# Second half's first mixer: selections made earlier, sparse queries projected last, sparse attention computed with queries on partitions

## The chip, the cores and the metric
The kernel runs on one core of a Trainium2 chip. The metric is the time of one execution on the device in microseconds (us): three runs of the kernel before took 3576.25 us in the median (3576.12 to 3578.21). The engines are TensorE (PE in the profile, with PEld for its weight loads), VectorE (DVE), ScalarE (ACT), GpSimd (POOL) and SyncE (SP), which issues most DMAs. Each works through its own list in order and waits on semaphores.

## The reference, cut to what matters
A first block of two layers (feed-forward, token mixer, feed-forward) is followed by a second block of two layers (mixer, cross attention, MLP). The change touches only the mixer of the second block's first layer, for 512 tokens and width 1024:

```
qa, ka, va, qb, ckv, qi, ki, wi = split(h @ w_in)
qa, ka = rope(rmsnorm(.)) per head (64 wide);  ki = rope(rmsnorm(ki));  qi = rope(qi)
kb, vb = split(rmsnorm(ckv) @ w_kv_up);  qb, kb = rope(rmsnorm(.)) per head
# dense part: 4 heads, each with two score maps, causal
attn  = softmax(qa0 ka0 / 8) - lam * softmax(qa1 ka1 / 8)
out_a = rmsnorm(attn @ va) * (1 - lam_init)
# sparse part: 8 heads; each query sees the 128 keys with the best index score
# (the loop of 16 rounds of 8 below), among those that are causal
isc   = sum_h relu(qi_h ki) * wi_h ;  idx = top_k(isc)
out_b = softmax(qb kb[idx] / 8) @ vb[idx]
y = concat(out_a, out_b) @ w_out
```

`rmsnorm` divides by the root of the mean square plus 1e-6 and multiplies by a gain per feature.

## The kernel before
Activations lie with features on partitions and the 512 tokens along the free dimension, in eight tiles of 128 features. A projection is computed from weights and activations that are each split in a high and a low part (`s_wh`, `s_wl`, `s_hh`, `s_hl`), with three matmuls for each product. The split of the weights costs ACT a copy (L1912) and DVE a subtraction (L2248) of 128x2048 for each chunk.

A planner (class `Plan`) writes one list of steps; every engine then executes its part of each step in this order. A projection calls `tick()` after each half of an output tile (12 matmuls of 512 columns). A tick advances each unit of background work in `active` by one stage and starts new ones from the queue `bg`, at most `burst` (1, in the sparse part 2), while fewer than `depth` are active and at least `reserve` scratch tiles are spare. `until` and `pipeline` tick with no projection beside. In this mixer `depth` is 7 (10 at the end) and `reserve` 3.

The order in `even_mixer` (L982): the projections of `qi`, `ki` and `wi`; then `qa`, `ka` (eight tiles), `va` with tokens on partitions, the compressed `ckv`, `qb` (four tiles), and the product of the normed `ckv` with `w_kv_up`, which gives `kb` and `vb`. The normed `ckv` is written into the tiles of `h` itself (`ck_part`), so it waits until the projection of `qb`, the last reader of `h`, has ended. The background queue holds in this order:
- `index` (L2660 to L2676): for the query blocks i = 1, 2, 3 the index scores of (i+1)*128 keys; 16 rounds of MAX8 (`ix_top`, L2669) and MATCH_REPLACE8 (L2671), which take out the eight best keys of each query at a time; and a mask `bm`. Block 1 does two rounds a tick, blocks 2 and 3 one round.
- `group(1)`, for `qa` and `ka`: `g_rs` computes the roots of eight heads' mean squares for each of `qa` and `ka` by Newton steps on DVE (L2224 to L2236). `g_turn` transposes them (L1804). For each of the eight tiles `g_scale` spreads the roots over the features with one PE matmul (`s_rt`) and multiplies them in on DVE (L2640); `e_rope` then turns the tile (PE, POOL L2898, DVE L2645 and L2647). `group(2)` does the same for `qb` and `kb`, once both are projected.
- 16 dense units (`a_unit`), 4 heads by 4 query blocks: two score matmuls (`s_ka`, `s_qa`), DVE adds the causal mask and takes the maximum (L2688), ACT computes exp and the sum (L2126). `ea_mix` takes two reciprocals, scales one map by its reciprocal (L2699) and adds the other (L2703). Then come transposes on PE (L1574), a copy on ACT and the product with `va`.
- `a_norm`: the mean squares of the dense output, roots, and their application (L2724).
- 32 sparse units (`attend`), in the order of head pair, query block, head: one score matmul of 64 rows (`s_kb`, `s_qb`); DVE adds the mask and takes the maximum (L2522); ACT computes exp and the sum (L2076); DVE takes the reciprocal (L2528) and scales the map (`at_norm`, L2530); PE transposes (L1574), ACT copies (L1912). In `at_av` PE multiplies by `vb`: the 64 features of a head are the stationary operand, 128 queries stream, and two heads of a pair write the lower and the upper 64 partitions of one bank. When a pair's four blocks are done the bank is split into the tiles 4 to 7 of `h` (ACT L1912, DVE L2241). The projection by `w_out_e` reads the tiles of `h` in the order 0 to 7.

Of the kernel before, what the change touches and what calls it, by code (L numbers as in the profile page):

```python
# [18 lines left out]
F32 = mybir.dt.float32  # L19
# [86 lines left out]
class Plan:  # L106
# [825 lines left out]
    def attend(self, kind, l, h, i, n, cell, last, free=None, sr=None):  # L932

        u = (kind, l, h, i)
        b, q, sm = self.banks.take(), self.tmp.take(), self.small.take()
# [3 lines left out]
        self.add("at_norm", u, n, q, sm)  # L939
        self.small.free(sm, ("at.n", u))  # L940
        yield
# [10 lines left out]
        if last:  # L952
            o = cell[0]
            if kind == "x":
                self.held.free(o, ("o.lo", l, h), ("o.hi", l, h))
            else:
                self.held.free(o, ("h.lo", self.hv, 4 + h // 2), ("h.hi", self.hv, 4 + h // 2))
# [24 lines left out]
    def even_mixer(self, norm):  # L982
        extra = [("xe", 0)]
        pend = []
# [21 lines left out]
        def proj(idx, key, t0, col, stat=True, eager=False):  # L1006
            ch = self.take("w_in_e", idx)
            for t, (b, pid) in enumerate(self.feat2(ch, 8, "h", hv, eager)):
                if t == 0:
                    flush()  # L1010
                self.add("e_copy", key, t0 + t, pid, b)
                if stat:
# [20 lines left out]
        def group(gid, n, tiles, turns=None):  # L1033
            y = self.yr.take()
# [7 lines left out]
            self.yr.free(y, ("g.t", gid))  # L1042
# [3 lines left out]
            for tile in turns or tiles:  # L1046
# [8 lines left out]
            yield  # L1055

# [11 lines left out]
        for i in extra:  # L1068
            self.tmp.after[i] = [free]
        self.tmp.ids += extra  # L1070
        self.reserve, self.depth = 3, 7
        self.add("e_begin")
        parts = []
# [31 lines left out]
        def index():  # L1105
            for i in (1, 2, 3):
# [22 lines left out]
        small = self.small.take()  # L1129
        self.add("e_gains", small)  # L1130
        for i, key in enumerate(("qa", "ka")):
            for c in range(2):
                proj(2 * i + c, key, 2 * c, 8 * i + 4 * c)
        for c in range(2):
            ch = self.take("w_in_e", 8 + c)
            for i in (0, 2):
# [3 lines left out]
                if i + c:  # L1140
                    continue
                flush()
                self.bg.append(group(1, 16, [(key, n) for key in ("qa", "ka") for n in range(4)],
                                     [(key, n) for n in range(4) for key in ("qa", "ka")]))
# [4 lines left out]
        def a_unit(h, i, cell):  # L1149
# [6 lines left out]
            self.add("ea_score", h, i, b, q, s)  # L1156
            yield
            self.add("ea_mix", h, i, q, s)
# [27 lines left out]
        proj(6, "ckv", 0, 0)  # L1186
        sq, pend[:] = list(pend), []
        held = []

        def compressed():  # L1190
            b = self.banks.take()
            self.add("ck_stat", [q for q, *_ in sq], b)
            for q, *_ in sq:
                self.tmp.free(q, ("ck.st",))
            yield
            y = self.yr.take()
            self.add("ck_rs", b, y, ew)
            self.banks.free(b, ("rs.v", "ck"))
            yield
            b, qs = self.banks.take(), [self.tmp.take(), self.tmp.take()]  # L1200
            self.add("ck_scale", y, b, qs)
            self.yr.free(y, ("ck.sp",))
            self.banks.free(b, ("ck.q", 1))
            yield
            held.extend(qs)

        self.active.append(compressed())
        for c in range(2):
            self.hfree = proj(4 + c, "qb", 2 * c, 4 * c)
        self.until(lambda: held)  # L1210
        self.hv += 1
        for k, q in enumerate(held):
            self.add("ck_part", k, q, self.hv, self.hfree)
            self.tmp.free(q, ("h.lo", self.hv, k), ("h.hi", self.hv, k))
        ch = self.take("w_kv_up", 0)
        cv = self.hv

        def vup(i):
            b, pid = self.toks(ch, 2, 1024, [i], "h", cv, 512, 512)
            self.add("e_vb", i, pid, b)  # L1220
# [4 lines left out]
        for n in range(4):  # L1225
            b, pid = self.feat(ch, 2, 1024, n, "h", cv)
# [4 lines left out]
            self.tick()  # L1231
        vup(0)
# [2171 lines left out]
```

## Time and profile before

| | |
|---|---|
| median of 3 runs | 3576.25 us (3576.12 to 3578.21) |
| profiled execution | 3573.11 us, span 3571.8 us |
| mean granted clock of TensorE | 0.983 |
| PE busy | 3463.5 us (97%) |
| DVE busy | 1880.2 us (53%) |
| ACT busy | 1189.9 us (33%) |
| POOL busy | 505.4 us (14%) |

The span runs from the first to the last instruction. The busy time of PE is modelled; the granted clock says in tenths or as a share of 1 which part of the full TensorE clock the chip granted. The mixer in question lies at about 2140 to 2470 us of the span.

### The profile page before, as it was taken

The page shows a single profiled execution, that of the slowest core. Times are in us where ns is not written, and L with a number is a line of the kernel's source. Part 1 is how long each engine was busy: PE and PEld are TensorE (multiplying, and loading weights), DVE is VectorE, ACT ScalarE, POOL GpSimd, SP SyncE. Part 2 cuts the span into 40 slices and gives each one's busy share as a digit, 9 for nine tenths or more (in the row PEclk, how much of TensorE's full clock was granted, in tenths as well). Part 3 has the DMA queues.
Part 4 walks back from the last instruction along what each step waited for, and adds up shares of the span by engine and source line. Part 5 has one row for each costly group of instructions (what it writes and reads, how often), then busy time and mean ns, then how long its engine had stood idle before and what let it go on. Part 6 is the DMA issues. An engine that isn't in the chain of part 4 may idle for free. (4 is left out here: it accounts for less than half of the span.)

```text
span 3571.8 us, 40973 instructions
## 1 busy us (share of the span) xinstructions
PE 3463.5 (97%) x16684; PEld 2814.3 (79%) x16684; DVE 1880.2 (53%) x3253; ACT 1189.9 (33%) x1611; POOL 505.4 (14%) x436
## 2 busy tenths in 40 slices
PE   8999989999999999999999999989999999999999
PEld 5888876788888888866788887656888888878887
DVE  5545745464556545745652345786554444564333
ACT  3222444342225222444342234235432222352221
POOL 1010212110012010211210021111111110211111
PEclk9999999999999999999999999989999999999999
DMA  6444221134442444321132212101222222322221
GB/s 263 176 173 177 101 77 60 59 118 153 158 149 106 153 153 159 105 73 54 69 134 99 97 66 83 56 16 48 83 83 95 95 95 96 111 75 90 102 94 71
DMA packets 56111, 377.56 MB, mean 106 GB/s; under 512 B 6897, under 2 KB 7025, under 8 KB 13170
## 3 DMA queue, kind: packets, MB, share of 16 engines
q1 hardware_dynamic: 55922, 374.93, 29.3%
q8 instruction: 132, 2.16, 0.2%
q14 instruction: 57, 0.47, 0.0%
HBM read 368.61 MB, written 2.10 MB: 104 GB/s over the span
## 5 line engine op out<-in xcount | busy, mean ns | idle before, releaser
L1554 PE MATMUL ps<-s_hh,s_wh 128*128 128x512 f32 x2488 | 992.6, 399 | 27.2 <-DVE s_xr L2303 10.5
L1554 PE MATMUL ps<-s_hh,s_wl 128*128 128x512 f32 x2488 | 977.1, 393 | 0.0
L1554 PE MATMUL ps<-s_hl,s_wh 128*128 128x512 f32 x2488 | 976.5, 392 | 0.0
L2248 DVE TENSOR_TENSOR s_wl<-s_stage,s_wh 128x2048 fp32r<-128x2048 f32 (+1 forms) x276 | 623.6, 2259 | 665.9 <-ACT s_wh L1912 665.8
L1912 ACT ACTIVATE s_wh<-s_stage 128x2048 fp32r<-128x2048 f32 (+1 forms) x276 | 519.1, 1881 | 600.2 <-PE ps L1554 456.5
L1554 PEld LDWEIGHTS ps<-s_hh,s_wh 128*128 128x128 f32 x2488 | 472.3, 190 | 146.8 <-issue 28.2
L1554 PE MATMUL ps<-s_ah,s_wh 128*128 128x512 f32 x1408 | 561.0, 398 | 0.3 <-POOL s_al L2864 0.3
L1554 PEld LDWEIGHTS ps<-s_hh,s_wl 128*128 128x128 f32 x2488 | 471.7, 190 | 101.1
L1554 PE MATMUL ps<-s_ah,s_wl 128*128 128x512 f32 x1408 | 549.1, 390 | 0.0
L1554 PEld LDWEIGHTS ps<-s_hl,s_wh 128*128 128x128 f32 x2488 | 472.7, 190 | 96.8 <-issue 1.2
L1554 PE MATMUL ps<-s_al,s_wh 128*128 128x512 f32 x1408 | 548.6, 390 | 0.0
L2864 POOL TENSOR_TENSOR s_al<-s_tmp,s_ah 128x512 fp32r<-128x512 f32 x152 | 197.4, 1301 | 1679.5 <-ACT s_ah L1912 1679.4
L1554 PEld LDWEIGHTS ps<-s_ah,s_wl 128*128 128x128 f32 x1408 | 263.7, 187 | 57.4
L1554 PEld LDWEIGHTS ps<-s_ah,s_wh 128*128 128x128 f32 x1408 | 264.1, 188 | 53.9 <-issue 1.4
L1554 PEld LDWEIGHTS ps<-s_al,s_wh 128*128 128x128 f32 x1408 | 264.2, 188 | 53.7 <-issue 1.9
L1912 ACT ACTIVATE s_ah<-s_tmp 128x512 fp32r<-128x512 f32 x152 | 95.9, 632 | 569.6 <-DVE s_tmp L2428 307.4
L2305 DVE TENSOR_TENSOR s_xr<-ps,s_xr 128x512 f32<-128x512 f32 x96 | 66.2, 689 | 197.1 <-PE ps L1554 197.0
L2264 DVE SCALAR_TENSOR_TENSOR s_tmp<-s_stage,s_cond,s_tmp 128x256 f32<-128x256 f32 x381 | 156.3, 478 | 0.0
L2303 DVE SCALAR_TENSOR_TENSOR s_xr<-ps,s_sm,s_xr 128x512 f32<-128x512 f32 x112 | 83.2, 748 | 115.7 <-PE ps L1554 115.1
L1940 ACT ACTIVATE s_tmp<-ps 128x512 f32<-128x512 f32 x82 | 48.9, 596 | 260.5 <-PE ps L1554 260.5
L2428 DVE TENSOR_TENSOR s_tmp<-s_tmp,ps 128x512 f32<-128x512 f32 x82 | 55.6, 685 | 117.5 <-PE ps L1554 116.3
L2412 DVE TENSOR_TENSOR s_tmp<-ps,s_c 128x512 f32<-128x512 f32 x64 | 44.1, 688 | 119.3 <-PE ps L1554 105.4
(489 smaller groups left out, 3720.6 us busy)
## 6 DMA issues: line engine op xcount, KB each, us to landing
s_stage<-in_w_ada SPq DMA_DIRECT2D x64, 1024.0 KB, 4.8
s_stage<-in_ffn_w_gate SPq DMA_DIRECT2D x44, 1024.0 KB, 4.8
s_stage<-in_ffn_w_up SPq DMA_DIRECT2D x44, 1024.0 KB, 4.8
s_stage<-in_ffn_down SPq DMA_DIRECT2D x32, 1024.0 KB, 4.8
s_stage<-in_w_up SPq DMA_DIRECT2D x32, 1024.0 KB, 4.8
s_stage<-in_down_m SPq DMA_DIRECT2D x32, 1024.0 KB, 4.7
s_stage<-in_w_in SPq DMA_DIRECT2D x24, 1024.0 KB, 4.8
s_stage<-in_ffn_down SPq DMA_DIRECT2D x16, 768.0 KB, 4.3
```

The lines of the kernel that those rows point to most:

```text
L1554: return pe.matmul(out, lhs, rhs, start=start, stop=stop, skip_group_check=True)
L1912: return act.activation(out, src, ACT.Copy)
L1940: act.activation(m.tmp(q), m.bank(b), ACT.Silu).then_inc(*e.up("act_ffn", "act", pid))
L2248: ins = dve.tensor_tensor(m.wl(ws)[:, a:z], m.STAGE[:, j % NS, a:z], m.wh(ws)[:, a:z].bitcast(F32), ALU.subtract)
L2264: ins = dve.scalar_tensor_tensor(dst, w[:, k, :], cond, dst, ALU.mult, ALU.add)
L2303: ins = dve.scalar_tensor_tensor(x, m.bank(b), m.small(gate[0])[:, n:n + 1], x, ALU.mult, ALU.add)
L2305: ins = dve.tensor_tensor(x, m.bank(b), x, ALU.add)
L2412: dve.tensor_tensor(x, m.bank(b), m.RB, ALU.mult).then_inc(*e.up("dve_act", "act", pid))
L2428: dve.tensor_tensor(m.tmp(q), m.tmp(q), m.bank(b), ALU.mult).then_inc(*e.up("dve_ffn", "glu", pid))
L2864: pool.tensor_tensor(m.AL[a][:, k, :], m.tmp(q), m.AH[a][:, k, :].bitcast(F32), ALU.subtract).then_inc(*e.up("pool_a", "a.lo", av, k))
```

## The change
The units' stages change, and the order of the projections. The rest of the kernel is the same.

```diff
 even_mixer (planner)
+        early = [("xv", k) for k in range(4)]        # the four tiles of vb as scratch, until vup
-        self.reserve, self.depth = 3, 7
+        self.reserve, self.depth = 4, 12             # and no self.depth = 10 later
         index:
                     self.add("ix_top", i, r, s)
-                    if i > 1 or r % 2:
+                    if r % 2:
                         yield
         order of projections
-        qa, ka, va (group 1 queued after its first half), ckv, qb, [ck_part], kb, vb, group(2: qb+kb)
+        qa, ka, ckv, [group 1 queued], va, [ck_part], kb, vb, group(2: kb), qb, queries()
         def queries():
+            self.add("g_rs", 3, 8, None, list(st["ev"]), ew)
+            done["minus"] = True
         def turned(tile):                            # for qa and qb, right after the copy
+            yield
+            rope(tile, ("e.p", *tile))
         b_units
-            for pr in range(4):
-                for i in range(4):
-                    for c in range(2):
-                        yield self.attend("b", 0, 2 * pr + c, i, (i + 1) * P, cell, ...)
+            for i in range(4):
+                for h in range(8):
+                    yield self.attend("b", 0, h, i, (i + 1) * P, cell, h == 7, sr=bs)
         attend
-        self.add("at_norm", u, n, q, sm)             # and its stage, for "b" only
+            elif kind == "b":                        # after the eighth head of a block
+                yield
+                self.add("b_norm", i, o, sr, q)
+                yield
+                self.add("b_turn", i, q, b)
+                self.add("b_out", i, b, self.hv, free or self.hfree)
 PE
+        if u[0] == "b":   # at_av: the transposed map is stationary, vb streams
+                ins = mul(m.bank(o)[:, 64 * u[2]:64 * u[2] + 64], m.tmp(p)[:, j * P:(j + 1) * P], m.v_of(u, j), ...)
+    def b_turn(i, q, b):
+        turn(m.bank(b), m.tmp(q), S).then_inc(*e.up("pe_turn", "b.t", i))
 ACT
+        if key in ("qa", "qb"):                      # e_copy
+            ins = act.activation(m.tile(key, t), m.bank(b), ACT.Identity, scale=m.small(gains[0])[:, at:at + 1])
+    def b_out: copy(m.HH[:, 4:8, i * P:(i + 1) * P], m.bank(b)...)
 DVE
     g_rs: groups 1 and 3 also write minus = -roots of the queries
     at_score, ea_score: tensor_tensor_reduce(..., ALU.add, ALU.min)
-      scale -1.0
+      scale m.minus(...)                             # minus the query's root, one number per partition
     ea_mix
-        dve.reciprocal(s0[:, 3:4], s0[:, 2:3])
-        dve.tensor_scalar(a0, a0, s0[:, 3:4], None, ALU.mult)
-        dve.tensor_tensor(s1[:, 4:5], s1[:, 3:4], m.LAM[:, 0:1], ALU.mult)
+        dve.tensor_scalar(s1[:, 4:5], s1[:, 3:4], m.LAM[:, 0:1], total, ALU.mult, ALU.mult)
     an_rs: eps becomes 1e-6 times the square of the sum (one instruction more)
+    def b_norm(i, o, sm, q):
+        dve.reciprocal(rc, rc)                       # 8 sums
+        dve.tensor_tensor(q, bank(o), rc broadcast over 64 columns, ALU.mult)
+    def b_out: dve.tensor_tensor(m.HL[:, 4:8, i * P:(i + 1) * P], m.bank(b), m.HH[...], ALU.subtract)
 memory
     the normed ckv goes to the place of qb (QBR) instead of the tiles of h
```

So `qa` and `qb` are no longer multiplied by their roots: the gain is applied in ACT's copy, the tile is turned at once, and the root comes in at the scores. The maps aren't normalized; a block's output of eight heads is multiplied by the reciprocal sums once, then transposed (four transposes) into the tiles 4 to 7 of `h`. Sparse units wait for `kb`, for `minus` and for the mask of block 1, and from block 2 on for their own mask; before they waited for the mask of block 2, and the first of block 3 for that of block 3.

## Rows read from the trace of the kernel before

**Rows 1.** Page, part 1: busy time, share of the span, instructions of each engine.
```profile
PE 3463.5 (97%) x16684; PEld 2814.3 (79%) x16684; DVE 1880.2 (53%) x3253; ACT 1189.9 (33%) x1611; POOL 505.4 (14%) x436
```
**Rows 2.** Stages: window, length, busy PE, PEld, DVE, ACT, POOL; clock, DMA share, GB/s.
```profile
2177.00:2214.00 37.00, 37.00 (x175) 29.22 (x173) 15.37 (x39) 18.16 (x26) 10.95 (x8) 0.91 0.16 57
2214.00:2297.00 83.00, 81.28 (x440) 59.98 (x440) 63.16 (x154) 26.22 (x47) 11.98 (x8) 1.00 0.18 63
2297.00:2357.00 60.00, 52.59 (x257) 39.69 (x253) 35.39 (x105) 26.03 (x56) 0.00 (x0) 0.89 0.11 37
2357.00:2430.00 73.00, 58.99 (x228) 34.28 (x228) 64.63 (x191) 22.72 (x65) 11.91 (x10) 0.77 0.00 1
2430.00:2469.00 39.00, 35.51 (x282) 23.56 (x280) 28.01 (x109) 27.22 (x83) 3.91 (x3) 1.00 0.00 1
2177.00:2469.00 292.00, 265.37 (x1375) 186.73 (x1373) 206.55 (x596) 120.35 (x277) 38.75 (x28) 0.91 0.10 33
```
**Rows 3.** Timeline 2293 to 2333: start, us, engine, line, instruction, idle before and releaser.
```profile
2299.55 0.72 ACT L2126 ACTIVATE s_tmp<-s_tmp,s_sm 128x512 f32<-128x512 f32 x1 [7.38 <-DVE s_sm L2688]
2302.09 0.50 PE L1554 MATMUL ps<-s_hh,s_wh 128*128 128x512 f32 x1 [4.39 <-ACT s_tmp L2107]
2329.45 0.48 PE L1554 MATMUL ps<-s_hh,s_wh 128*128 128x512 f32 x1 [2.51 <-DVE s_hl L2241]
```
**Rows 4.** Busy time in stretches of 2.5 us, columns as in rows 2.
```profile
2330.00:2332.50 2.50, 2.50 (x9) 2.04 (x8) 1.56 (x1) 1.30 (x2) 0.00 (x0) 0.50 0.00 0
2475.00:2477.50 2.50, 2.50 (x13) 2.07 (x12) 0.00 (x0) 1.99 (x7) 1.04 (x2) 1.00 0.97 338
```
**Rows 5.** PE timeline: start, us, instruction; each with the one that follows.
```profile
2384.54 1.12 PE L1554 MATMUL ps<-s_rt,s_c 16*128 16x512 f32 x2
2385.59 1.12 PE L1554 MATMUL ps<-s_qb,s_cc 128*128 128x512 f32 x2
2386.55 1.05 PE L1554 MATMUL ps<-s_tmp,s_va 128*128 128x128 f32 x8
2387.44 0.38 PE L1574 MATMUL ps<-s_cc,s_xe 128*128 128x128 f32 x2
2408.15 1.05 PE L1554 MATMUL ps<-s_cc,s_xe 128*128 128x1 f32 x8 [1.20 <-ACT s_xe L2148]
2409.13 0.49 PE L1554 MATMUL ps<-s_kb,s_qb 64*128 64x128 f32 x4
2454.91 1.36 PE L1574 MATMUL ps<-s_cc,s_ka 128*128 128x128 f32 x8 [0.61 <-DVE s_ka L2530]
```
**Rows 6.** Instructions on `vb` alone, 2177 to 2469: PE, PEld, ACT, clock.
```profile
2177.00:2469.00 292.00, 15.12 (x160) 11.49 (x160) 2.34 (x4) 0.91 0.10 33
```
**Rows 7.** DVE line 2530 alone, 2177 to 2469.
```profile
2177.00:2469.00 292.00, 12.38 (x32) 0.91 0.10 33
```
**Rows 8.** DVE line 2699 alone, 2177 to 2469.
```profile
2177.00:2469.00 292.00, 7.14 (x16) 0.91 0.10 33
```
**Rows 9.** DVE by line and form, 2177 to 2469: busy, mean ns, idle before.
```profile
L2669 DVE MAX8 s_sm<-s_bm 128x8 f32<-128x512 f32 x16 | 11.0, 690 | 0.1
L2671 DVE MATCH_REPLACE8 s_bm<-s_sm,s_bm 128x512 f32<-128x512 f32 x16 | 10.8, 676 | 0.0
L2528 DVE RECIPROCAL s_sm<-s_sm 128x1 f32<-128x1 f32 x32 | 5.1, 159 | 2.8 <-ACT s_tmp L2076 1.6 <-ACT s_ka L2076 0.9 <-ACT s_qi L2076 0.3
L2640 DVE SCALAR_TENSOR_TENSOR s_qb<-s_qb,s_sm,ps 128x512 f32<-128x512 f32 x4 | 3.0, 738 | 0.0
L2241 DVE TENSOR_TENSOR s_hl<-ps,s_hh 128x512 fp32r<-128x512 f32 x3 | 2.1, 692 | 4.1 <-ACT s_hh L1912 4.1
```
**Rows 10.** Timeline: the last of the 12 DVE instructions of a chain of roots.
```profile
2422.29 0.17 DVE L2236 SCALAR_TENSOR_TENSOR s_ny<-s_nu,s_ny 128x16 f32<-128x16 f32 x1
```
**Rows 11.** ACT by line and form, 2409 to 2469.
```profile
L2076 ACT ACTIVATE s_ka<-s_ka,s_sm 128x128 f32<-128x128 f32 x4 | 1.6, 394 | 0.8 <-DVE s_sm L2522 0.8
L1912 ACT ACTIVATE s_tmp<-ps 128x128 f32<-128x128 f32 x6 | 1.3, 262 | 0.0
```

More of the change, by code:

```diff
@@ L934, in attend @@
         u = (kind, l, h, i)
-        b, q, sm = self.banks.take(), self.tmp.take(), self.small.take()
+        b, q, sm = self.banks.take(), self.tmp.take(), sr if kind == "b" else self.small.take()
         self.add("at_score", u, n, b, q, sm, sr)
@@ L1031, in root, with group @@
             done["ew"] = True
-        def group(gid, n, tiles, turns=None):
-            y = self.yr.take()
+        def group(gid, n, tiles):
+            y = self.yr.take() if gid == 0 else None
             self.add("g_rs", gid, n, y, list(st["ev"]) if gid else [("e.stt", 0)], ew)
@@ L1045, in group @@
             prev = None
-            for tile in turns or tiles:
+            for tile in tiles[4:] if gid == 1 else tiles:
                 b = self.banks.take()
@@ L1055, in group, with turned @@
             yield
+        def turned(tile):
+            yield
+            rope(tile, ("e.p", *tile))
         def rope(tile, before):
@@ L1133, in even_mixer, with compressed @@
                 proj(2 * i + c, key, 2 * c, 8 * i + 4 * c)
+        proj(6, "ckv", 0, 0)
+        sq, pend[:] = list(pend), []
+        held = []
+        self.bg.append(group(1, 16, [(key, n) for key in ("qa", "ka") for n in range(4)]))
+        def compressed():
+            b = self.banks.take()
+            self.add("ck_stat", [q for q, *_ in sq], b)
+            for q, *_ in sq:
+                self.tmp.free(q, ("ck.st",))
+            yield
+            y = self.yr.take()
+            self.add("ck_rs", b, y, ew)
+            self.banks.free(b, ("rs.v", "ck"))
+            yield
+            b, qs = self.banks.take(), [self.tmp.take(), self.tmp.take()]
+            self.add("ck_scale", y, b, qs)
+            self.yr.free(y, ("ck.sp",))
+            self.banks.free(b, ("ck.q", 1))
+            yield
+            for k, q in enumerate(qs):
+                self.add("ck_part", k, q)
+                self.tmp.free(q, ("c.lo", 0, k), ("c.hi", 0, k))
+            held.extend(qs)
+        self.active.append(compressed())
         for c in range(2):
@@ L1184, in even_mixer @@
         self.bg.extend(a_units())
[L1186 to L1207, printed above, removed]
-        for c in range(2):
-            self.hfree = proj(4 + c, "qb", 2 * c, 4 * c)
         self.until(lambda: held)
[L1211 to L1214, printed above, removed]
         ch = self.take("w_kv_up", 0)
-        cv = self.hv
+        self.tmp.ids = [i for i in self.tmp.ids if i not in early]
         def vup(i):
-            b, pid = self.toks(ch, 2, 1024, [i], "h", cv, 512, 512)
-            self.add("e_vb", i, pid, b)
+            b, pid = self.toks(ch, 2, 1024, [i], "c", 0, 512, 512)
+            self.add("e_vb", i, pid, b, self.tmp.after["xv", i])
             self.banks.free(b, ("vb", i))
@@ L1231, in even_mixer, with queries @@
             self.tick()
+        self.until(lambda: not self.tmp.busy.intersection(early))
         vup(0)
         flush()
-        self.active.append(group(2, 16, [(key, n) for key in ("qb", "kb") for n in range(4)]))
+        self.active.append(group(2, 8, [("kb", n) for n in range(4)]))
         for i in (1, 2, 3):
-            self.hfree = vup(i)
-        self.release(ch, self.hfree)
+            last = vup(i)
+        self.release(ch, last)
+        for c in range(2):
+            self.hfree = proj(4 + c, "qb", 2 * c, 4 * c)
+        flush()
+        def queries():
+            yield
+            self.add("g_rs", 3, 8, None, list(st["ev"]), ew)
+            st["ev"].clear()
+            done["minus"] = True
+        self.active.append(queries())
         self.hv += 1
@@ L1536, in up, with same @@
         return (self.book.sems[sem], by) if self.live else (None, by)
+    def same(self, event, *others):
+        for other in others:
+            self.book.at[other] = self.book.at[event]
 def xe(n, v):
@@ L2504, in at_score @@
     def at_score(u, n, b, q, sm, sr):
-        mx, nm = m.small(sm)[:, 0:1], m.small(sm)[:, 1:2]
-        e.wait_ge(("at.s", u), sm.after)
+        mx, nm = m.small(sm)[:, 0:1], m.max_sum(u, sm)[0]
+        e.wait_ge(("at.s", u), [("b.n", u[3] - 2)] if u[0] == "b" and u[3] > 1 else sm.after)
         if u[0] == "x":
```

213 lines of the change are left out of this document (136 added, 77 removed).

## The prediction, made before the change was run
> **What bounds the kernel now.** I read the page's busy times first: PE is busy for 97% of the span, DVE for 53%, ACT for 33% [rows 1]. So only PE's work, its pauses and its clock count. The table by stage [rows 2] says where the mixer differs: of the 292 us from 2177 to 2469 PE is busy for 265.4, so 26.6 are pauses, and the clock is below 1 in three of five stages. Busy time times the missing share of the clock is lost as well. By stage, pauses plus clock: 0 + 3.3 us, 1.7 + 0, 7.4 + 5.8, 14.0 + 13.6, 3.5 + 0. That is 49.3 us; the work itself, at the full clock, is 242.7 us. The reader is to see how the stages differ: from 2214 to 2297 DVE works for 76% of the time and PE loses 2%; from 2357 to 2430, with no projection left, DVE works for 89% and PE loses 27.6 of 73 us.
>
> The timeline [rows 3] shows how a busy DVE reaches PE: at 2299.55 ACT had waited 7.38 us for a maximum of DVE (behind a weight split, selections and a root chain), and PE, whose banks ACT empties, stood for 4.39 us. The second pause of this kind, 2.51 us before 2329.45, is the wait for the parts of `ckv`, which may overwrite `h` only after the last `qb` matmul. Right behind it the clock is at 0.50, the lower of its two levels, 1.2 GHz [rows 4].
>
> **PE's work.** (1) The spreading matmuls of `qa` and `qb` go: eight, each 1.05 us from its start to the next (2384.54 to 2385.59) [rows 5]: -8.4 us. (2) The 80 products with `vb` (160 records) keep their number; they took 15.1 us [rows 6], 0.094 us a record, because two heads share the array in halves of its columns. After, 128 columns are stationary, 64 stream, and nothing runs beside it. The trace has no such form. Its neighbours with 128 stationary columns take 0.11 us a record with 128 streaming (0.89 us for eight) and 0.12 with one (0.98 for eight) [rows 5]: 17.8 to 19.6 us. If only the stream counted, half of 0.11 would give 8.9 us. The two neighbours agree although their streams differ by 128 times, so the load decides; I take 18.6: +3.5 us (-6.2 to +4.5). (3) New are 16 transposes, 0.15 us each (eight in 1.36 with their drain) [rows 5]: +2.4 us. Work after: 242.7 - 8.4 + 3.5 + 2.4 = 240.2 us.
>
> On (2) the Trainium skill, TensorEngine Tiling (Array Packing), section "Performance Considerations", speaks against the change: with a streaming side of at most 64 one should swap the operands and tile the columns twice, which is what the kernel before does. Its factor of two would make 30.2 us of the 15.1; it is the last rival below.
>
> **DVE's work.** Removed: the 32 scalings of sparse maps, 12.4 us [rows 7], their 32 reciprocals, 5.1 [rows 9]; the 16 dense scalings, 7.1 [rows 8], with 16 reciprocals of 0.16, 2.5; eight applications of roots at 0.738, 5.9 [rows 9]. Together 33.0. Added: four output norms (0.69 for 128x512, by the split's row, and 0.16), 3.4 us; a third chain of roots, twelve instructions of 0.17 to 0.21, 2.4 [rows 10]; three small ones, 0.6. The four splits of the output replace four of the same size. The multiply by `minus` replaces an immediate in the same instruction: taken as 0; at most one small instruction of 0.16 for each of 64, 10 us of DVE. Net -26.6: 206.6 becomes 180 us, against 240 of PE.
>
> ACT gets a gain in a copy that it makes anyway, at nothing: it is busy for 120 of 292 us [rows 2], and even 0.1 us for each of eight is hidden behind the tile's own matmuls. POOL's part of the turning is unchanged and only comes earlier. SP issues nothing more; weight chunks are read in another order.
>
> **The order, up to the sparse part.** Without the sparse part (80 transposes 12.5, products 18.6, the new turns 2.4, scores some 12: pairs of 128 columns take 0.41 to 0.45, those of 512 about 1; together 45 us) PE has 195 us. DVE has 160 (180 less some 14 for maxima, estimated from the scalings' 12.4 at the same widths, and 6 for norms and splits): 82%, between the two stages above, which lost 2% and 38%. What changes the mix: two rounds of selection a tick instead of one, so `index` takes 30 ticks instead of 46 and ends before `qb` is projected, whose four tiles load PE but hardly DVE; the queries are turned without waiting for roots; `ckv` no longer waits for `qb`, so the pause of 2.51 us and most of the 5.8 us of clock behind it go. Against it: the two rounds of block 3 take 2 x (0.690 + 0.676 + the 0.09 load) = 2.9 us of DVE a tick [rows 9], while a half tile takes PE 12 x 0.227 = 2.7 (2.5 us hold 11 new matmuls and two that reach in) [rows 4]; and the ticks beside `kb` and `vb` are shorter than that. Over some 180 us I take a loss of 9%, 16 us, where it was 42.5; the bounds are 2% and what it was, 3.6 to 42.5. The 3.3 us before 2214 stay.
>
> **The sparse part.** It starts when `qb`'s last tile is copied, squared (0.6 us each), summed, rooted (2.4) and negated; the first units then need DVE and ACT once. Some 7 us, of which turning the last tile and late dense units cover 2: 5 us of pause that was not there (0 to 10). What is queued behind it is everything on PE, and `w_out_e` waits for that. Blocks 0 and 1 come as eight small units each. For block 0 ACT needs 0.394 for exp, 0.1 for the sum that is not overlapped and 0.262 for the copy, 0.76 a unit [rows 11], PE 0.6 (score 0.22, transpose 0.15, product 0.23): 1.3 us over eight; for block 1, with PE at 1.08 (0.32, 0.30, 0.46), they are equal. I take 3 us for both. In the large blocks PE waited for the scaling (0.61 at 2454.91 [rows 5]), which goes: 2.5 us of pauses instead of 3.5. The last `b_turn` waits for `b_norm` with nothing between: 0.69 and two signals, 1.2 us; earlier ones have the next block's units. The copy and subtraction behind the last turn, 0.6 and 0.69 us, lie beside the matmuls on tiles 0 to 3 of `h`, 24 x 0.227 = 5.4 us; if `a_norm` were late, they would cost 1.5 us.
>
> **Sum.** 240.2 + 3.3 + 16 + 5 + 3 + 2.5 + 1.2 = 271.2 us for 292: -20.8. The profiled execution took 3573.11 us, its span 3571.8, the median is 3576.25; taken from the median, this is 3555.5: I predict 3556 us.
>
> **Rivals.** (A) *DVE no longer holds PE at all.* For it: 76% of DVE cost PE only 2% [rows 2]. Against it: DVE's work is still bunched where index, dense units and `kb` meet. The loss is 5 us, the pause 2: 257.2 us, -35: 3541.
> (B) *The bunching moves and stays.* The selections, twice as dense, meet the weight splits, the turning and the dense units, and ACT waits for maxima as at 2299.55 [rows 3]. For it: 2.9 against 2.7 us a tick. Against it: DVE has 26.6 us less. The loss is 33 us instead of 16, all else as in the sum: 288, -4: 3572.
> (C) *Slower: PE runs dry at the start of the sparse part and stays at the low clock.* The selections being done early, nothing is left to fill the root chain; PE stands for 10 us, and the small units of blocks 0 and 1, PE work of 13.4 us in bursts, run at 1.2 GHz and take as much again. For it: the clock was 0.50 behind the pause at 2329 [rows 4] and 0.77 over the stage of short bursts [rows 2]. Against it: the dense units, five ticks long, reach into the `qb` projection. With 25 us lost earlier: 240.2 + 3.3 + 25 + 10 + 16.4 + 3.7 = 298.6, +6.6: 3583. It decides from 18 us of earlier loss on.
> (D) *The products with `vb` cost twice.* 30.2 us instead of 18.6, all else as in the sum: -9: 3567. Against it: eight records with 128 stationary columns took 0.89 us.
>
> **How the numbers follow.** Forecast 0.42, A 0.20, B 0.18, C 0.12, D 0.08. What this kernel's measurement can tell from no change is 0.2%, 7 us. Forecast and A are faster, as are 0.05 of B and half of D: 0.71. The rest of B and D is the same: 0.17. C is slower: 0.12. The range runs from A, 3541, to just past B, 3575, and leaves out C and the lower edge of A. The forecast's own range, with half of each unknown, is 3547 to 3565.
>
> **What would show it.** Right: `s_rt` spreads nine tiles instead of seventeen; records on `vb` stay 160 at 0.11 us and start one after the other; DVE falls by about 27 us; the last MAX8 lies more than 30 us before the first sparse score; no pause before the `kb` matmuls, and one of about 5 us behind the last `qb` matmul. Wrong: pauses plus lost clock between 2214 and the sparse part above 25 us, a low clock in blocks 0 and 1, or records on `vb` above 0.15 us.

## The result, and the profile after

The changed kernel takes 3592.4 us in the median of five runs (3591.5 to 3593.6), the kernel before 3577.1 beside it: a ratio of 1.0043, interval 1.0033 to 1.0054. It is slower by 15.3 us; the prediction was 3556 and faster. The profiled execution of the kernel before (3573.11 us) was quicker than its median by 4 us, so the two profiles lie 18.6 us apart, 3 more than the medians.

The page of the changed kernel, part 1, answers to [rows 1]:

```profile
PE 3464.7 (96%) x16684; PEld 2826.3 (79%) x16684; DVE 1865.4 (52%) x3171; ACT 1193.2 (33%) x1611; POOL 504.8 (14%) x436
```
The span is 3590.4 us, 18.6 longer, and PE is busy for 1.2 us more: the time went into pauses. The stages of the changed kernel, columns as in [rows 2]; the sparse part starts at 2422, the first projection matmul behind it at 2484.6 (2409 and 2469.1 before):

```profile
2178.00:2214.00 36.00, 34.17 (x166) 26.10 (x165) 19.09 (x44) 18.54 (x26) 15.70 (x11) 0.97 0.17 59
2214.00:2287.00 73.00, 71.30 (x412) 57.27 (x411) 55.61 (x136) 20.46 (x33) 6.91 (x5) 1.00 0.16 59
2287.00:2345.00 58.00, 42.48 (x172) 26.13 (x171) 49.31 (x129) 21.33 (x48) 2.53 (x2) 0.85 0.10 37
2345.00:2422.00 77.00, 56.20 (x258) 40.20 (x258) 42.23 (x116) 26.63 (x66) 7.60 (x6) 0.83 0.04 14
2422.00:2484.60 62.60, 59.62 (x380) 45.94 (x379) 26.91 (x92) 36.54 (x105) 5.08 (x4) 0.86 0.00 1
2177.00:2484.60 307.60, 264.77 (x1385) 196.45 (x1385) 193.45 (x516) 124.49 (x279) 37.81 (x28) 0.89 0.09 31
```
From 2287 to 2422, dense units beside the last projections, PE stands for 36 of 135 us. The longest pauses of PE there, from its timeline (columns as in [rows 3]), and one of ACT:

```profile
2295.72 1.87 PE L1585 MATMUL ps<-s_cc,s_tmp 128*128 128x2 f32 x8 [4.36 <-ACT s_tmp L2163]
2335.78 2.07 PE L1585 MATMUL ps<-s_rt,s_c 8*128 8x512 f32 x2 [4.41 <-DVE s_kb L2719]
2338.26 0.51 ACT L2183 ACTIVATE s_ki<-s_ki,s_sm 128x256 f32<-128x256 f32 x1 [7.95 <-DVE s_sm L2767]
2347.42 0.80 PE L1585 MATMUL ps<-s_hh,s_wh 128*128 128x512 f32 x1 [5.47 <-ACT s_tmp L2163]
2368.39 0.77 PE L1585 MATMUL ps<-s_hh,s_wh 128*128 128x512 f32 x1 [6.42 <-ACT s_xe L2163]
2396.04 1.86 PE L1585 MATMUL ps<-s_cc,s_ki 128*128 128x2 f32 x8 [4.54 <-ACT s_ki L2163]
2408.92 0.47 PE L1605 MATMUL ps<-s_cc,s_tmp 128*128 128x128 f32 x1 [5.14 <-DVE s_tmp L2778]
2421.24 1.05 PE L1585 MATMUL ps<-s_cc,s_tmp 128*128 128x1 f32 x8 [1.20 <-ACT s_tmp L2205]
```
Four of them end with ACT's square of a projected tile (L2163, `e_sq`): the first among the `kb` matmuls, two directly ahead of query matmuls (`s_hh`, `s_wh`), whose bank ACT had not emptied, and the one at 2396.04 behind the last query matmul, for the sums of the last query tile. The timeline of all engines ahead of 2368.39, in order:

```profile
2358.68 0.69 DVE L2748 MAX8 s_sm<-s_bm 128x8 f32<-128x512 f32 x1
2361.00 0.68 DVE L2750 MATCH_REPLACE8 s_bm<-s_sm,s_bm 128x512 f32<-128x512 f32 x1
2361.70 1.26 POOL L2979 TENSOR_TENSOR s_qb<-s_qb,s_c 128x512 f32<-128x512 f32 x1
2362.31 1.20 DVE L2726 TENSOR_TENSOR s_kb<-s_kb,s_tmp 128x512 f32<-128x512 f32 x1
2364.14 0.69 DVE L2726 TENSOR_TENSOR s_qb<-s_qb,s_tmp 128x512 f32<-128x512 f32 x1
2365.25 0.75 DVE L2778 SCALAR_TENSOR_TENSOR s_qi<-s_ki,s_sm,s_qi 128x512 f32<-128x512 f32 x1
2365.92 0.34 DVE L2767 CUSTOM_DVE_ANT_0 s_tmp<-ps,s_cc,s_minus 128x128 f32<-128x128 f32 x1
2366.31 0.40 ACT L2183 ACTIVATE s_tmp<-s_tmp,s_sm 128x128 f32<-128x128 f32 x1 [5.09 <-DVE s_sm L2767]
2367.10 0.67 ACT L2156 ACTIVATE s_qb<-ps,s_sm 128x512 f32<-128x512 f32 x1
2367.67 0.58 ACT L2163 ACTIVATE s_xe<-ps 128x512 f32<-128x512 f32 x1
```
This is one step of the plan. DVE does two rounds of block 3 (2358.7 to 2361.6), the turning of a key and of a query tile (behind POOL), a mix, and then the dense maxima, 7.2 us after the step began. ACT waits 5.09 us for them, does the exponentials, and only then the copy and square of the query tile; PE had gone idle at 2361.97.

The pause of 5.14 us before 2408.92 has another length of list ahead of it. The selections have long ended (last MAX8 at 2373.8). PE waits for the mix of a dense unit, and that stands on DVE behind the root chain of the queries, 2.9 us from its first instruction to the end of `minus`:

```profile
2405.23 0.18 DVE L2695 TENSOR_TENSOR s_nv<-s_st,s_sm 128x32 f32<-128x32 f32 x1
2407.92 0.18 DVE L2707 TENSOR_SCALAR s_minus<-s_roots 128x32 f32<-128x32 f32 x1
2408.51 0.35 DVE L2778 SCALAR_TENSOR_TENSOR s_tmp<-s_tmp,s_sm 128x128 f32<-128x128 f32 x1
```

For each kernel I added up windows of 1 us, from 2177 to the first matmul of `w_out_e`: idle is length less busy, lost clock is busy time by the missing share of the clock, work is the rest.

| mixer | idle | lost clock | work of PE | DVE busy | rest of the kernel, lost clock |
|---|---|---|---|---|---|
| before (292.1 us) | 26.6 | 24.6 | 240.9 | 206.5 | 5.1 |
| changed (307.6 us) | 42.8 | 25.9 | 238.9 | 193.5 | 8.3 |

The pauses (+16.2) are the result. PE's work fell by 2.0, 1.3 more of clock were lost in the mixer, and 3.2 more behind it.

### The profile page after: what moved, and what is told of

Its sections match the earlier page's. It is cut to its first block, busy times and chain, and to the rows that moved or that the text cites. A ratio compares the mean times of both kernels' runs of the same rounds, so it can differ in the third digit from the quotient of the medians.

```text
span 3590.4 us, 40926 instructions
## 1 busy us (share of the span) xinstructions
PE 3464.7 (96%) x16684; PEld 2826.3 (79%) x16684; DVE 1865.4 (52%) x3171; ACT 1193.2 (33%) x1611; POOL 504.8 (14%) x436
## 4 chain that ended last, share of the span: by engine, by line
PE 44%; DVE 4%; ACT 1%; issue 1%; POOL 0%; DVEq 0%; ACTq 0%; POOLq 0%
PE ps L1585 43%; PE ps L1605 1%; DVE s_bm L2750 0%; DVE s_sm L2748 0%; DVE s_wl L2305 0%; ACT s_wh L1954 0%; ACT s_tmp L2118 0%; DVE s_xr L2434 0%; DVE s_tmp L2767 0%; DVE s_sm L2565 0%; DVE s_hl L2298 0%; ACT s_xx L2118 0%; DVE s_na L2287 0%; DVE s_nu L2289 0%; DVE s_tmp L2424 0%
## 5 line engine op out<-in xcount | busy, mean ns | idle before, releaser
L1585 PEld LDWEIGHTS ps<-s_ah,s_wh 128*128 128x128 f32 x1408 | 264.9, 188 | 53.7 <-issue 1.4
```

The lines of the kernel that those rows point to most:

```text
L1585: return pe.matmul(out, lhs, rhs, start=start, stop=stop, skip_group_check=True)
```

## The experiments

Five runs or more for each, all beside the kernel before (3576.7 to 3577.9 us in the comparisons). "Late" is the change's order (queries last), "early" has the queries ahead of the expansion.

**One selection round a step (late, new form).**
```diff
-                    if r % 2:
+                    if i > 1 or r % 2:
```


> The changed kernel with one round of selections a step of the plan for blocks 2 and 3 (two for block 1), as the kernel before had it. Everything else is the change's: queries last, new order, folded factors, new sparse form. (The row buffer of the sparse maxima and sums lies in a place of its own, as one buffer more is then in use.) Theory D, the dense: the added idle time (42.8 us against 26.6 between 2177 and the last projection) comes from two selection rounds (2.9 us for block 3) standing in VectorE's queue ahead of the dense maxima of the same step, ScalarE waiting for those maxima with the eviction of a query projection behind it, and TensorE behind that. Then this kernel is 8 to 15 us faster than the changed one: 3577 to 3584 us. Theory O, the order of the projections: the pauses come from the late query projections lying beside the dense units, whatever the selections do: 3590 to 3596 us. Theory S, the new sparse form costs it: 3592 us, within 2.


3581.5 us, ratio to before 1.0014 (1.0005 to 1.0023): 11 us less than the changed kernel. Mixer: idle 30.1, clock 26.1. So two rounds do cost, in this order. (The sparse maxima and sums got a row buffer of their own here, as one buffer more is in use at a time.)

**Selections last in a step.**
```diff
-        self.active = [u for u in self.active if next(u, "end") != "end"]
+        order = [u for u in self.active if u is not last] + [u for u in self.active if u is last]
+        self.active = [u for u in order if next(u, "end") != "end"]
```


> The changed kernel with the unit that issues the selections advanced last in each step of the plan, so that VectorE has the dense maxima and mixes of a step ahead of its two selection rounds. Same work, same number of steps. Theory D: most of the 16 us of added idle time goes, 3578 to 3584 us. Theory O: no more than 3 us, 3589 to 3592 us. Theory S: 3592 us. Slower, 3595 us or more, if what ends last after all are the selections of block 3, which then come later.


3587.4 us, 1.0030 (1.0018 to 1.0041): 5 us less than the changed kernel. Idle 36.2. A part, smaller than expected; that the next step's maxima then stand behind them may be why, which no run tells.

**The old sparse form and order (late).** `attend`, `at_norm`, `at_turn`, `at_av` and `b_units` as before, scale `minus` kept.
```diff
-                ins = mul(m.bank(o)[:, 64 * u[2]:...], m.tmp(p)[:, j * P:...], m.v_of(u, j), ...)
+                ins = mul(m.o_of(u, o), m.v_of(u, j), m.tmp(p)[:, j * P:...], ...)
```


> The changed kernel with the sparse units of the kernel before: rows normed one by one (reciprocal and multiply on VectorE), value products with features on partitions, four pairs of heads one after another, no turn of the outputs. The queries' scale stays with the maximum. Theory S, the new form of the products (21.2 us of TensorE against 15.1, 16 turns more, low clock in the sparse part 8.5 us against 6.5) costs what was lost: 3577 to 3582 us. Theories D and O: the loss was before the sparse part, so that this one is as slow as the changed kernel or slower by the 13 us of VectorE's work that comes back where VectorE bounds: 3590 to 3604 us.


3585.1 us, 1.0022 (1.0013 to 1.0031): 7.3 us less than the changed kernel. PE's work in the mixer is 233.2 instead of 238.9, idle unchanged (43.6), although DVE has 13.5 us more. So the new form costs its work on PE, and what it spares DVE is worth nothing. The edit undoes the swap, the 16 turns and the order by blocks together; no run parts them. The products' weight loads and matmuls, first of the changed kernel, then of this one (duration in ns: least, median, most):

```profile
L1585 PEld LDWEIGHTS ps<-s_vb,s_ka x46: 186/192/333, 2434.9 to 2480.9; 128*128 128x128 f32 x46
L1585 PE MATMUL ps<-s_vb,s_ka x46: 222/275/421, 2435.1 to 2481.0; 128*128 128x64 f32 x46
```
```profile
L1571 PEld LDWEIGHTS ps<-s_ka,s_vb x64: 132/137/231, 2437.3 to 2478.7; 128*64 128x64 f32 x64
L1571 PE MATMUL ps<-s_ka,s_vb x64: 272/273/476, 2437.3 to 2478.8; 128*64 128x128 f32 x64
```
The matmuls last the same with half the stream; the load of 128 columns takes 192 ns instead of 137, and the tile is the whole array. Over a run of each kind, from the timelines of both:

```profile
2460.74 1.45 PE L1585 MATMUL ps<-s_vb,s_tmp 128*128 128x64 f32 x12
```
```profile
2457.14 1.36 PE L1571 MATMUL ps<-s_ka,s_vb 128*64 128x128 f32 x14
```
From the start of each run to the start of what follows it that is 0.108 us a record (2460.74 to 2462.03, twelve) against 0.094 (2457.14 to 2458.65, sixteen in all), both at the full clock.

**Queries early (new form, two rounds).** The projection of `qb` and `queries()` move ahead of `w_kv_up`; the split `ckv` goes to `h` again.
```diff
+        for c in range(2):
+            self.hfree = proj(4 + c, "qb", 2 * c, 4 * c)
+        flush(); self.active.append(queries())
         self.until(lambda: held)
+        self.add("ck_part", k, q, self.hv, self.hfree)     # into h
         kb, vb, group(2: kb)
-        qb, queries()
```


> The changed kernel with the sparse queries projected ahead of the expansion of the compressed part, as in the kernel before, the split compressed part back in the normed input's place. Two selection rounds a step, folding and new sparse form stay. The dense units can then start beside the query projections (16 of 16 scored by the end of the projections' last value tile but 6, against 9). Theory O: 3576 to 3583 us. Theory D: two rounds a step lie ahead of the dense maxima as before, 3588 to 3593 us. Theory S: 3592 us.


3574.3 us, 0.9993 (0.9984 to 1.0002): 18 us less than the changed kernel, though `ckv` waits for the queries again. Idle 29.6, clock 19.5. With two rounds, the order is the largest part.

**Early, with one round; then with the old form; then old form with two rounds.**


> Queries projected ahead of the expansion and one selection round a step for blocks 2 and 3; folding and the new sparse form stay. Queries early alone gave 3574.3 (18 us less than the changed kernel), one round alone 3581.5 (11 less). If the two causes are separate (theory O and D both true), this kernel takes 3564 to 3570 us. If both are one cause, a step overfull beside the late query projections, the second step adds little: 3572 to 3576 us. Slower than 3576 us if the selections of block 3, drawn out again, now end last before the sparse units of that block.

> As the last, and the sparse units in their old form and order: what is left of the change is the folding of the factors into the exponents and maxima, the values' space lent as scratch, and the late maxima waiting for the factors. Old form alone saved 7.3 us on the changed kernel (5.7 us less TensorE work). Theory S as an additional, separate cost: 6 to 8 us less than the last one, 3558 to 3564 us. If VectorE bounds instead (13.5 us of its work come back), no less than the last one: 3566 to 3572 us. The kernel before takes 3576.7.

> As the last but with two selection rounds a step for blocks 2 and 3. It says what the early selections alone do once order and sparse form are the old ones: theory D 4 to 10 us slower than the last one (3564 to 3572), theory of one cause 0 to 2 us slower.


3581.3, 3576.9 and 3563.5 us; to before 1.0010 (1.0002 to 1.0019), 1.0001 (0.9993 to 1.0010), 0.9962 (0.9948 to 0.9975). One round is slower here than two (by 7 us with the new form, by 13 with the old); of what I had written down only the last case of the first expectation allowed for it. The two causes are not separate. Two rounds, early and the old form beat both kernels.

**The kernel before with two rounds.**
```diff
-                    if i > 1 or r % 2:
+                    if r % 2:
```


> The kernel before with one edit: two selection rounds a step for blocks 2 and 3, which brings the last selection from step 57 of the plan to step 42. VectorE's work is the same 206.5 us. Theory D (bunched selections ahead of the dense maxima hold ScalarE and TensorE back): 3580 to 3588 us against 3576.7. Prediction's view (the selections go into time in which TensorE has work of its own, the loss shrinks): 3568 to 3574 us.


3587.3 us, 1.0026 (1.0015 to 1.0037), 10 us slower: with nothing else of the change, early selections lose, as the rival to the prediction's view had it. Its longest pauses:

```profile
2310.26 0.79 PE L1554 MATMUL ps<-s_hh,s_wh 128*128 128x512 f32 x1 [6.86 <-ACT s_tmp L2107]
2348.26 0.77 PE L1554 MATMUL ps<-s_hh,s_wh 128*128 128x512 f32 x1 [8.71 <-DVE s_hl L2241]
```
They are the two of [rows 3], 4.39 and 2.51 us there. These two grew by 8.7 us, but other pauses shrank: over the mixer idle is 28.9 (2.3 more), lost clock 28.5 (3.9 more) and the busy time at full clock 245.0 (4.1 more, with the same matmuls, which nothing here explains). So the pauses alone are not the 10 us.

**The late order with the old form and one round.**


> The changed kernel with the old sparse form and one round a step. It fills the last corner: late or early queries, one or two rounds, with the old form. With the new form late queries cost nothing at one round (3581.5 against 3581.3). Theory V says the same here: 3573 to 3580 us against 3576.9 with early queries. If the equality was chance, late queries cost 5 us or more here too: 3582 us and up.


3574.0 us, 0.9992 (0.9983 to 1.0001). The corners (medians, us):

| | late, two rounds | late, one | early, two | early, one |
|---|---|---|---|---|
| new form | 3592.4 (the change) | 3581.5 | 3574.3 | 3581.3 |
| old form | 3585.1 | 3574.0 | 3563.5 | 3576.9 |

Late costs 18 and 22 us with two rounds, 0 and -3 with one. The new form costs 4 to 11 us in each column.

Where the time is lost, from the same windows of 1 us (pauses + lost clock, us). The cut is at the last projection matmul ahead of the sparse units: of `vb` in the kernel before and in the early ones, of `qb` in the late ones.

| | 2214 to the last projection | from there to the first sparse score | sparse part |
|---|---|---|---|
| before | 10.7 + 6.7 | 7.9 + 7.9, in 45.1 us | 8.0 + 6.5 |
| the change (late, two) | 26.0 + 9.5 | 12.0 + 6.2, in 34.2 us | 3.0 + 8.5 |
| late, one (new form) | 9.1 + 6.0 | 14.7 + 9.9, in 45.1 us | 4.6 + 9.2 |
| early, two (new form) | 20.3 + 9.2 | 3.7 + 0.0, in 22.2 us | 3.0 + 8.5 |
| early, one (new form) | 15.6 + 11.1 | 7.0 + 4.7, in 34.0 us | 5.1 + 8.9 |

Two rounds in the late order lose ahead of the last projection (20.4 us more than one) and give 6.4 back behind it. The late order with two rounds loses 6.0 us ahead of it and 14.5 behind it, where the last query tile's square, the root chain and the dense units' rest stand one behind the other; with one round the late order also costs 12.9 there, but gives 11.6 back ahead of it. Dense units move across this cut from kernel to kernel, so that the table says where the loss lies and not what each unit costs.

**Is it room for dense units to start?** `self.reserve` 2 instead of 4 in the changed kernel; and no lent scratch (`early = []`) in the 3563.5 kernel.


> The changed kernel, queries late, with one number changed: a new unit starts when 2 scratch tiles are free (the change asks for 4). By the last query matmul step 14 dense units have had their scores instead of 11, and the sparse units begin 2 steps earlier. Theory P (pacing: what the early queries bought was room for dense units to start, 18 us): 3574 to 3582 us, near the kernel with early queries. Theory O (the late query projections, whose evictions and squares stand in ScalarE's queue behind dense exponentials, are the pauses themselves): 3588 to 3595 us, the five pauses of 4.4 to 6.4 us stay.

> The fastest so far (early queries, old sparse form, two rounds a step: 3563.5 us) without the four scratch tiles lent from the values' place, so that 9 instead of 13 dense units have their scores by the end of the projections. Theory P: 8 to 15 us slower, 3572 to 3578. Theory O: order alone did it, within 3 us, 3561 to 3567.


3591.5 us, 1.0041 (1.0027 to 1.0055), and 3564.5 us, 0.9965 (0.9953 to 0.9978). Neither made the difference that pacing would. `depth` 12 instead of 7 was not tried alone.

**The keys out of the query steps (late, two rounds).**
```diff
-        self.active.append(group(2, ...kb))        # after vup(0)
+        self.active.append(group(2, ...kb))        # after the projection of qb
```


> The changed kernel, queries late and two rounds, but the roots, scaling and rotation of the sparse keys begin when the query projections have ended instead of beside them. Open: why late queries cost 18 us with two rounds and nothing with one. Theory V (a step's queue on VectorE is too long: beside a query projection it holds two rounds of block 3, 2.9 us, the scaling and rotation of a key tile, the rotation of a query tile, and only then the dense maxima; the pauses of 4.4 to 6.4 us end with the square behind those maxima): without the keys in it the steps are 2 to 3 us shorter, and this kernel takes 3576 to 3584 us. Theory Q (the queries' own evictions and squares behind dense exponentials are enough): 3589 to 3596 us, or more, as the keys now come last.


3589.9 us, 1.0037 (1.0025 to 1.0050): 2.5 us less than the changed kernel. That is far from theory V and within what theory Q said. Its pauses:

```profile
2331.62 0.47 PE L1605 MATMUL ps<-s_cc,s_tmp 128*128 128x128 f32 x1 [4.07 <-DVE s_tmp L2778]
2358.15 0.48 PE L1605 MATMUL ps<-s_cc,s_ki 128*128 128x128 f32 x1 [5.82 <-DVE s_ki L2778]
2383.24 1.86 PE L1585 MATMUL ps<-s_cc,s_tmp 128*128 128x2 f32 x8 [4.53 <-ACT s_tmp L2163]
```
The two pauses ahead of the query matmuls, 11.9 us, are gone, but others came, of transposes that wait for DVE's mixes: idle 36.0 (6.8 less) and clock 28.8 (2.9 more). Without the keys in those steps the two pauses do not occur, but nearly half of their length comes back elsewhere, and behind the last query matmul 11.8 us of pauses and 7.9 of clock are lost (12.0 and 6.2 in the changed kernel).

**Only block 3 with one round (late, new form).** `if i == 3 or r % 2`; the dense and projection steps stay what they are.


> The changed kernel with one round a step for block 3 alone. The other work falls into the same steps of the plan as in the changed kernel, step by step up to the sparse units; only the 32 selections of block 3 (22 us of VectorE) lie over 16 steps instead of 8, and end ahead of the sparse units. It is the cleanest test of the two rounds: if they, queued ahead of the dense maxima beside the query projections, cost the 11 us that one round for both blocks gave back, 3578 to 3584 us, with the two pauses of 5.5 and 6.4 us ahead of the query matmuls under 3 us each. If it was block 2's rounds, or room for other units: 3588 to 3593 us.


3584.6 us, 1.0022 (1.0013 to 1.0031): 7.8 us less than the changed kernel, with nothing moved up to the sparse units but the 16 rounds of block 3 (a row buffer of its own, as in the one-round kernel, beside it). Idle 35.7. The two pauses ahead of the query matmuls are

```profile
2340.30 0.80 PE L1584 MATMUL ps<-s_hh,s_wh 128*128 128x512 f32 x1 [3.41 <-ACT s_tmp L2162]
2360.94 0.76 PE L1584 MATMUL ps<-s_hh,s_wh 128*128 128x512 f32 x1 [5.86 <-ACT s_xe L2162]
```
3.41 (5.47) and 5.86 (6.42) us: the first lost some of its length, the second hardly, against the expectation; its step also holds both turnings.

**Both together.**


> As the last with the keys' roots, scaling and rotation after the query projections. Held back alone they gave 2.5 us (idle time 6.8 less, lost clock 2.9 more). If the step's length on VectorE is what counts, both together are at least as good as the last one, 3574 to 3581 us; if the keys at the end are a chain of their own, 2 us or more slower than it.


3584.4 us, 1.0021 (1.0012 to 1.0031). Idle in the mixer fell to 30.4, 5.3 below the last one, but the clock lost 14.9 us behind the mixer instead of 5.1, with the same work there. Time for time nothing was gained, and neither account is confirmed by it.

**Towards a better version**, all early, old form, two rounds (3563.5). (a) `a_norm` runs beside the sparse units instead of ahead of them; (b) also selections last in a step; (c) a, with one round for block 3; (d) a, without lent scratch.


> Early queries, old sparse form, two rounds, and the sparse units no longer queued behind the norm of the dense outputs: they start as soon as the keys are ready, the norm runs beside them when the last dense head is done. Takes 2 of 70 steps out of the plan, at its thinnest place (16.4 us between the last dense and the first sparse score, where TensorE had 1.7 and 1.2 us pauses and a lowered clock). 4 to 9 us less than 3563.5: 3555 to 3560. If the drain is bound by VectorE's norm of the dense outputs and its queue, no change: 3562 to 3565.

> As the last, and the selections issued last in each step, behind the dense maxima. On the changed kernel that gave 5 us. Theory D says 2 to 5 us less than the last one (3552 to 3558); if the pauses left (4.1, 3.1, 4.3, 4.5 us) are of another cause, within 1.5 us of it.

> Early queries, old sparse form, sparse units not queued behind the norm (3563.4), and one round a step for block 3 alone, two for blocks 1 and 2. Its last selection then comes 8 steps later, at the step in which the sparse units begin, 3 steps ahead of its first use. Theory V: each of 8 crowded steps has 1.45 us less ahead of its dense maxima, and the two pauses of 4.3 and 4.5 us shrink: 3555 to 3561 us. If what one round lost in the same order (3576.9 against 3563.5) was the selections of block 3 as such: 3566 to 3575 us.

> Early queries, old sparse form, two rounds, no lent scratch, sparse units not queued behind the norm. Each of the last two edits alone left 3563.5 within 1 us. 3559 to 3565 us; the best candidate for a version ahead of both kernels, with the fewest edits to the kernel's memory.


3563.4, 3565.0, 3567.7 and 3562.0 us (0.9962, 0.9967, 0.9975, 0.9961, each within 0.0014). (a) gained nothing against 3563.5 us, where I expected 4 to 9 us. Only (c) may be worse, against the expectation; its interval (0.9964 to 0.9985) still overlaps the others'. In its profiled execution the mixer had 2 us less idle and 12 us more lost clock than in that of (a); but that execution was its slowest of eight (3572.1 us), and that of (a) its fastest of five (3561.7), so the two profiles overstate the difference. The last one, 0.9961 (0.9949 to 0.9974), is as good as any: about 15 us ahead of the kernel before and 30 ahead of the changed one. It keeps of the change the folded factors, the early selections, `ckv` ahead of `va`, and `reserve` and `depth`.

## Why the prediction was wrong, step by step

- **PE's work**: predicted -2.5, measured -2.0. `s_rt` fell from 20.9 us to 11.0, nine tiles instead of seventeen as foreseen. The products with `vb` took 21.2 us, not 18.6, which is above the bound of 19.6. At the full clock they took the 0.11 us a record that the neighbours gave (0.108); the first of them ran at the low clock. The new form as a whole was put at +5.9 us of work (products and turns), and undoing it gave 5.7 back. The rule of the Trainium skill, TensorEngine Tiling (Array Packing), section "Performance Considerations", pointed the right way: undoing the swap, with the turns and the order that belong to it, gave 4 to 11 us. Its full factor of two (30.2 us) is not what the trace shows, 21.2 us.
- **DVE**: predicted -26.6, measured -13.1 busy. By the sum of the durations it is -20.0: the scalings, their reciprocals and the eight applied roots went as said (17.5 and 5.9), `ea_mix` by 8.1 instead of 9.6, and the multiply by `minus`, "taken as 0", is 3.9 us. The rest is overlap: the records of successive instructions overlap, and busy time counts that once (23.5 us before, 16.4 after). The size did not matter; with the old form DVE has 13.5 us more and the kernel is faster.
- **The loss up to the sparse part, the step that failed.** "I take a loss of 9%, 16 us, where it was 42.5": up to the last query matmul, where the next term begins, the loss was 26.0 us of pauses and 9.5 of clock, 35.5. The 42.5 was no fair start either: it runs to 2430, and the kernel before had 17.4 us up to its last projection matmul and 33.2 up to its first sparse score. I set the loss by DVE's mean share (82%, between two stages). The share from 2214 to the first sparse score even came out lower (147 of 208 us, 71%; 76% before), and the loss rose from 33.2 to 53.7. What the timelines point to is the length of DVE's list within a step ahead of the maxima that ACT waits for, as ACT has the next eviction behind them: spreading the rounds of block 3 gave 7.8 us, moving the selections to the end of a step 5, taking the keys out 2.5. Each is less than I expected of it. I had the figures, 2.9 us of rounds against 2.7 of a half tile, and used them against the mean only. I counted as a gain that `index` "ends before `qb` is projected": it ended beside it (last selection at 2374, query copies 2346 to 2395), since I didn't lay the steps side by side.
- **The start of the sparse part failed as well.** "5 us of pause that was not there (0 to 10)": from the last query matmul (2388.0) to the first sparse score (2422.2) PE stood for 12.0 us, and 6.2 us of clock were lost. The pauses are 4.54, 5.14, 0.43, 0.62 and 1.20 us. I had taken the late dense units as work that fills the wait for the root chain; their mixes stood behind that chain on DVE.
- **"No pause before the `kb` matmuls"**: right, the 2.51 us and the wait for `h` went, though a pause of 4.36 us came among those matmuls. The order that bought them cost 18 us.
- **Small and large blocks, tail**: 3.0 us of pauses instead of 6.7 (3, 2.5 and 1.2), but 8.5 us of lost clock, of which I had none, though the kernel before lost 6.5 there. The clock was 0.50 to 0.56 from 2422 to 2437. That 11.5 came near 6.7 is partly luck.
- **The sum**: 271.2 us became 307.6. Of the 36.4 us, 19.5 are the loss up to the last query matmul, 13.2 the stretch behind it, 4.8 the sparse part; PE's work was 1.3 less than foreseen. Of the signs named beforehand as wrong, two came: pauses plus lost clock above 25 us, and a low clock in blocks 0 and 1.
- **Rivals.** No one rival was right; the kernel did what B and C say, both at once. B's mechanism (selections twice as dense, ACT waits for maxima) and its price are seen up to the last query matmul, 35.5 us against 33. C had the sign and the stand at the start of the sparse part, 12.0 us against 10, and the low clock in the first blocks; for the whole sparse part it had 20.1 us where 11.5 were lost, and 25 of earlier loss. I gave C 0.12.

Shown: within the changed kernel the late order and two rounds cost only together (18 and 11 us; with one round the late order costs nothing, and in the early order two rounds gain); the new form costs PE work; lent scratch in the early order and the reserve in the late one do not matter. Seen in the traces, and only in part confirmed: that the length of DVE's list in a step is what makes the pauses. Open: why with early queries two rounds are better than one by 7 to 13 us, and in the kernel before, whose queries are early too, worse by 10. The folded factors, `ckv` ahead of `va`, the later place of `group(1)` and `depth` differ there, and none was tried alone. The profiles of the two early pairs say this much: with one round the mixer loses 6.5 (new form) and 5.2 us (old) more of clock; idle is the same in the new form, and in the old one it is 5.0 more, nearly all in the sparse part (8.0 us against 3.3), where the last selections then lie.

## What to carry to other kernels

Where engines walk one written list, add up for each step what stands on the slower engine ahead of the result that the next one waits for, and compare it with the bound engine's work in that step; a mean share over the stage says nothing of it. Parts of a reordering have no value of their own: early selections were worth -10, -11, +7 or +13 us depending on what else the kernel had of the change, so a change of several parts is tried in its corners. Here 13.5 us of DVE's work spared was not worth 5.7 us more on PE, which was the bound. And look at what stands behind the last projection: a chain that only the last tile can start has little beside it.

## What the runs showed of the hardware

- A custom DVE instruction (mask and maximum) with one scalar for each partition in place of an immediate takes 0.062 us more at every width: 0.748 against 0.686 us for 512 columns, 0.350 against 0.285 for 128. First of the changed kernel, then of the kernel before:

```profile
L2580 DVE CUSTOM_DVE_ANT_0 s_tmp<-ps,s_cc,s_minus 128x128 f32<-128x128 f32 x4 | 1.3, 350 | 7.7 <-PE ps L1585 7.7
L2767 DVE CUSTOM_DVE_ANT_0 s_tmp<-ps,s_cc,s_minus 128x512 f32<-128x512 f32 x4 | 2.8, 748 | 0.5 <-PE ps L1585 0.5
```
```profile
L2688 DVE CUSTOM_DVE_ANT_0 s_tmp<-ps,s_cc 128x128 f32<-128x128 f32 x8 | 2.0, 285 | 0.0
L2688 DVE CUSTOM_DVE_ANT_0 s_tmp<-ps,s_cc 128x512 f32<-128x512 f32 x6 | 3.9, 686 | 0.6 <-PE ps L1554 0.6
```
- The clock behind the mixer differed in the same part of the program. The 50 us that begin 50 us behind the mixer, first of the kernel before, then of the one with early queries and the new form (columns as in [rows 2]):

```profile
2519.10:2569.10 50.00, 49.63 (x329) 45.20 (x328) 31.36 (x78) 21.74 (x31) 5.19 (x4) 1.00 0.37 126
```
```profile
2515.70:2565.70 50.00, 49.62 (x321) 45.94 (x320) 30.88 (x73) 20.11 (x28) 5.16 (x4) 0.93 0.33 116
```
PE is as busy, yet the granted clock is 0.93 and 3.4 us are lost. Over the rest of the kernel 5.1 to 14.9 us were lost, from profile to profile. Executions of one kernel differ too: of the early one with the new form, four at a mean clock of 0.983 took 3572.7 to 3573.4 us, and three at 0.981 took 3575.4 to 3575.5, so that a difference of some 5 us between two kernels needs its clock looked at before it is given a cause.
